# A two-block network on one core: activation chunks of the matmul operands laid out at 1072 and 1088 bytes instead of 1024

## What is computed

```python
h = h + hybrid_mixer(rms_norm(h, norm_mix_g), w_in, ..., w_out)
h = h + memory_cross_attention(rms_norm(h, norm_xa_g), rms_norm(mem, norm_mem_g), xa_wq, xa_wk, xa_wv, xa_wo)
h = h + squared_relu_mlp(rms_norm(h, norm_mlp_g), mlp_w1, mlp_w2)      # D_FF = 8192
...                                                                    # second block, other weights
x = x + gt1 * (concat([o_mla, o_na, o_fn]) @ w_out)
x = x + gt2 * conv_ffn(h2, w_up, conv_w, conv_b, w_down)               # D_FF_2 = 5632
```

## Time and profile before

| | |
|---|---|
| time, median of 3 runs | 3139.58 us (3137.08 to 3141.41) |
| the profiled execution | 3139.84 us, span 3138.0 us |
| TensorE busy, matmul and weight load | 2968.9 us (95%) and 2905.4 us (93%) |
| VectorE busy | 2101.9 us (67%) |
| ScalarE busy | 1331.6 us (42%) |
| mean granted TensorE clock | 0.971 |
| bytes moved, mean rate | 591.58 MB, 189 GB/s |

### The profile page before, as it was taken

The page is one execution under the profiler, slowest core; times in us unless marked ns, Lnnn a source line. Parts: engine busy times, 40 slices in busy tenths (PEclk is TensorE's granted clock), DMA queues, the critical chain, the costliest instruction groups (busy, mean ns, idle before and its releaser), DMA issues.

```text
span 3138.0 us, 55206 instructions
## 1 busy us (share of the span) xinstructions
PE 2968.9 (95%) x23858; PEld 2905.4 (93%) x23858; DVE 2101.9 (67%) x2934; ACT 1331.6 (42%) x1646; POOL 5.1 (0%) x13
## 2 busy tenths in 40 slices
PE   7999788999999899999999989979998999999998
PEld 7999788999998899999999979959498999999998
DVE  6988654688877777676776775445456665665565
ACT  3445323343433443444435444435344444444443
POOL 0000000000000000000000000000000000000000
PEclk9999898999999999999999989998899999999999
DMA  5555102577655677777777734514054555556553
GB/s 199 176 174 162 54 1 103 175 268 256 242 202 182 245 277 276 276 280 264 282 268 262 280 133 168 182 61 134 21 181 144 180 194 186 185 188 195 182 188 115
DMA packets 160451, 591.58 MB, mean 189 GB/s; under 512 B 17840, under 2 KB 17840, under 8 KB 159696
## 3 DMA queue, kind: packets, MB, share of 16 engines
q1 hardware_dynamic: 159264, 579.93, 53.2%
q0 software_dynamic: 944, 8.12, 0.7%
HBM read 585.88 MB, written 2.10 MB: 187 GB/s over the span
## 4 chain that ended last, share of the span: by engine, by line
PE 87%; DVE 9%; ACT 3%; issue 1%; DMA 0%; SPq 0%; DVEq 0%; ACTq 0%
PE bank L446 77%; DVE wlo L1216 2%; PE bank L710 1%; DVE ev L1235 1%; DVE modacc L1421 1%; PE bank L467 1%; PE bank L461 1%; PE bank L614 1%; DVE tmp L1371 1%; PE bank L471 1%; PE bank L612 1%; PE bank L606 1%; PE bank L685 1%; DVE ev L1338 1%; ACT whi L821 1%
## 5 line engine op out<-in xcount | busy, mean ns | idle before, releaser
L446 PE MATMUL bank<-act,whi 128*128 128x256 f32 x10144 | 1856.5, 286 | 54.3 <-DVE wlo L1216 15.3
L446 PEld LDWEIGHTS bank<-act,whi 128*128 128x128 f32 x10144 | 1603.9, 195 | 59.2 <-issue 33.7
L1216 DVE TENSOR_TENSOR wlo<-raw,whi 128x1024 fp32r<-128x1024 f32 x906 | 1102.2, 1223 | 572.0 <-ACT whi L821 565.6
L446 PE MATMUL bank<-act,wlo 128*128 128x256 f32 x5072 | 1446.9, 285 | 0.0
L821 ACT ACTIVATE whi<-raw 128x1024 fp32r<-128x1024 f32 x906 | 948.1, 1057 | 946.3 <-PE bank L446 944.1
L446 PEld LDWEIGHTS bank<-act,wlo 128*128 128x128 f32 x5072 | 986.3, 194 | 0.0
L446 PE MATMUL bank<-hid,whi 128*128 128x256 f32 x3456 | 597.1, 278 | 0.0
L446 PEld LDWEIGHTS bank<-hid,whi 128*128 128x128 f32 x3456 | 524.7, 188 | 0.0
L446 PE MATMUL bank<-hid,wlo 128*128 128x256 f32 x1728 | 480.0, 278 | 0.0
L1202 DVE SCALAR_TENSOR_TENSOR modacc<-modraw,small,modacc 128x512 f32<-128x512 f32 x480 | 348.2, 746 | 11.8 <-DMA modraw<-mods 6.6
L446 PEld LDWEIGHTS bank<-hid,wlo 128*128 128x128 f32 x1728 | 324.8, 188 | 0.0
(11 more groups left out here) (269 smaller groups left out, 1520.8 us busy)
## 6 DMA issues: line engine op xcount, KB each, us to landing
raw<-stream SPq DMA_DIRECT2D x906, 512.0 KB, 4.4
modraw<-mods SPq DMA_DIRECT2D x192, 512.0 KB, 4.2
h<-x_t SPq DMA_DIRECT2D x4, 512.0 KB, 6.8
memV<-mem_t POOLq DMA_DIRECT2D x1, 2048.0 KB, 9.3
tmp<-ctx_t POOLq DMA_DIRECT2D x1, 2048.0 KB, 12.2
out_t<-tmp SPq DMA_DIRECT2D x4, 512.0 KB, 2.6
cz<-catt POOLq DMA_DIRECT2D x1, 1216.0 KB, 12.9
bias<-na_bias POOLq DMA_DIRECT2D x1, 1024.0 KB, 5.5
```

The lines of the kernel that those rows point to most:

```text
L446: mm = pe.matmul(b[:, hf * T:(hf + 1) * T], lhs, rhs, start=(kc == 0 and hf == 0 and n == 0), stop=(kc == ph.chunks - 1 and n == 2), skip_ ...
L1216: ve.tensor_tensor(wlo[:, at % SPL_N, :], raw[:, at % RAW_N, :], whi[:, at % SPL_N, :].bitcast(F32), ALU.subtract).then_inc(split_done, 1)
```

## The change

Three tensors get another shape. `act` has 268 columns in place of 256 for each chunk, `hid` has 272, and both are then cut to the first 256, so that all code that uses them is as it was; a chunk now starts 1072 bytes after the one before it in `act`, and 1088 bytes in `hid`. `act` takes 1536 bytes more of each partition, `hid` 2048, and `small` takes 256 less, which its users don't reach. No instruction is added or removed; every tensor behind `act` moves by 1536 bytes, and every one behind `small` by 1280.

```diff
-        act = sb("act", [P, 2, DC, T], F32R)
+        act = sb("act", [P, 2, DC, T + 12], F32R)[:, :, :, 0:T]
...
-        small = sb("small", [P, 256])
+        small = sb("small", [P, 192])
...
-                hid = sb("hid", [P, 2, DC, T], F32R, stack=mlp)
+                hid = sb("hid", [P, 2, DC, T + 16], F32R, stack=mlp)[:, :, :, 0:T]
```

## The result

The changed kernel takes 3120.58 us (median of 5, 3120.2 to 3123.64), the kernel before beside it 3137.08 us. The ratio is 0.9947, with a 95% interval of 0.9933 to 0.9962: 0.5% faster, 17 us, where I had forecast 65. It lies inside the stated range of 3032 to 3152 and on the forecast side of no change, but the gain is a quarter of what was predicted.

The account below looks back on a forecast made before the run. TensorE's matmul pace, set by operand addresses, was taken to bound the kernel. Gains of 55.9, 7.2 and 1.6 us on `act`, 0 for `hid` and the rest, sum to 64.7: 3139.8 to 3075 us, range 3032 to 3152.

Parts of the forecast that it names:

- What bounds the kernel: Line 446 matmuls: TensorE, 95% busy, sets the time; 120 ns on `act`, 113.3 or 117.5 on `hid`, by operand addresses.
- The pace on `act`: Line 446 matmuls on `act`: 120 ns falls to 115 with the new stride, 55.9 us less over 466 slots.
- I take no change: `hid` slots in `w2` and `down`: new stride and start cost 0 us, between 15 us less and 19 more.
- VectorE as the next bound: 224 `act` slots: VectorE binds from 86 to a little over 90% busy, so only 7.2 and 1.6 us gained.
- Half are bad: Cost goes by distance modulo 128 or so; `act` 117.5, `hid` about 117: 3111 us; 0.15 together with VectorE's rival.
- VectorE takes it back: TensorE at 115 ns, but VectorE or ScalarE binds in more phases: half the gain, 3108 us; 0.15 shared.
- Nothing: Operand place doesn't make the 120 ns, or it goes by distance modulo 64: time stays 3140 us; chance 0.11.
- Slower: the changing distance breaks the step: Load and matmul streams never settle: 4.2 ns more a matmul, 70 us on `act`, 14 on `hid`: 3223 us; 0.14.
- All distances but 0 are good: Only 0 modulo 512 is bad; `act` and `hid` both run at 113.3 ns: 100 us less, 3040; chance 0.12.

Follow-up runs that it names:

- the scan: Kernel without the network, only line 446's weight loads and matmuls, 168 at each fixed operand distance: 113.3 to 120.0 ns a matmul over 16 places, mean 117.9.
- the kernel with distance 112: Against the kernel before: chunk strides of 1024 bytes kept, `act` starts 112 bytes later, `hid` 48, both at distance 112 modulo 256; 3039.22 us, ratio 0.9683.

## Why the prediction was right and wrong

**What bounds the kernel: right.** TensorE's pace by operand address carried 15.2 of the 17.2 us; both strides moved the pace, and no other engine's busy time changed by more than 1.2 us.

**The pace on `act`: mis-sized.** The step that failed is "I take 115. It is nearer to the `hid` rows since that is the one distance that isn't 0". It is 118.4, near the upper of the two values that I had from rows. The trace of before had two distances, 0 and 448, and these are one of the three worst and one of the two best of 16. I took the good one for the usual one. The pattern visits all 16 places equally often, so it gets their mean, 117.9 in the scan, and half a nanosecond for the short stay. At 118.4 the term of the sum is 466 x 24 x 1.6 ns = 17.9 us, and those phases measured 19.4. The step from slots to time was sound; the pace that went into it was not.

**`hid`: "I take no change" was wrong.** I had the bounds -15 and +19 and it was +10.8 (3.2 in `w2`, 7.6 in `down`). The row at hand said that `hid` stood well and that the change moves 12 of its 16 chunks off that place (modulo 256; by the modulo 512 of the prediction it is 14); the four places that it visits now have 113.3, 120.0, 117.8 and 118.7 in the scan, a mean of 117.4, and 117.0 was measured. Taking the middle of a range was no reading of the row. The bounds were off too: the 2.84 us of a slot in `w2` hold the line-461 matmuls, and I set them against slots without any. With 113.3 throughout, in the kernel with distance 112, `w2` is 8.0 us shorter and `down` the same, so the lower bound was -8; the upper one, with 120 ns throughout, is about +27 by the same paces, an estimate.

**VectorE as the next bound: wrong for most of the 224 slots.** I gave `glu`, `z`, `memk`, `memv` and `wq` less than half of the gain and `wo` nearly none, because VectorE was busy for 86 to 90% of a window. For `wo` I had misread the row. The window of the earlier trace rows runs to 1060, and `wo` ends at 1056:

```profile
1000.00:1056.00 56.00, 56.00 (x470) 55.95 (x468) 50.49 (x64) 21.09 (x22) 0.00 (x0) 1.00 0.74 253
1056.00:1060.00 4.00, 1.21 (x10) 0.97 (x8) 2.14 (x4) 0.90 (x2) 0.00 (x0) 1.00 0.96 387
```

All the 2.79 us in which TensorE stood still lie behind the phase, so that row shows no bound by VectorE. Whole phases say the same. `wo`, from its first to its last matmul, in the kernel before and in the one with distance 112:

```profile
958.70:1056.00 97.30, 97.26 (x800) 97.22 (x800) 85.96 (x108) 36.34 (x38) 0.00 (x0) 0.98 0.69 243
```

```profile
938.50:1029.30 90.80, 90.69 (x800) 90.50 (x799) 85.17 (x109) 36.16 (x38) 0.00 (x0) 1.00 0.73 261
```

The same 800 matmuls (32 of them are short ones of line 461), 6.5 us less or 0.20 us a slot, where the pace alone gives 0.16; the rest, 1.4 us, is a shorter wait in its first slot. VectorE goes from 88% to 94% of the phase. `glu` and `z` gave 0.10, `memk` and `wq` 0.16. Only `qkv` kept its time, 0.7 us less in 48 slots. From 60 to 280 us of the kernel before, ScalarE waited longest for this:

```profile
ACT qkvT L858 <- DVE ev L1235: 51.0, 11, 5.6
```

There ScalarE and VectorE hand a bank to each other, and ScalarE's next split stands behind that wait. So `qkv` was bound with VectorE at 86%; that this chain is the cause is my reading of the waits and the code, and no run takes it apart. So the share didn't tell the phases apart. At 118.4 ns this error was small (6.7 us gained in those 224 slots where my shares at that pace would give about 3), and it partly made up for the `hid` term.

**The rivals.** "Half are bad" came nearest, at 3111 with 117.5 for `act` and 117 for `hid` against the measured 118.4 and 117.0; I gave it 0.15 together with "VectorE takes it back". I had argued its mechanism by "modulo 128 or so", and the scan shows 256. "Nothing", which rested on the rule of the Trainium skill ("TensorE: Matmul & The Clock Gate", Part 2) that a weight load takes no read bandwidth from the running matmul, falls: with all other engines idle the pace goes from 113.3 to 120.0 by where the two operands stand, and it matters where the load's own operand starts. So the place has an effect. Whether it is read bandwidth that one takes from the other is not shown: that the two reads meet in the memory is a guess of mine, and no run here shows what happens inside. "Slower: the changing distance breaks the step" falls for `act`, whose patterns cost 0.4 ns by changing. The two paces of the earlier trace rows that it was built on are real: they are the two states of place 192. In the `w2` windows of the changed kernel there is no second pace, perhaps because no chunk stays at 192 for long; no run tests that. "All distances but 0 are good" falls by the scan, where 14 of 16 places are slower than 113.3. "VectorE takes it back" falls as well: it needed TensorE at 115, and in `up_1` TensorE never stood still and had 118.4.

**The sum.** Forecast were 55.9 us for the 466 slots, 8.8 for the other 224 on `act`, and 0 for `hid`. Measured are 19.4 (36 less, by the pace: 17.9 at 1.6 ns for 55.9 at 5), 6.7, and -10.8; with 2.0 between the phases that is 17.2, but for rounding. So the time landed in the range by a pace on `act` that gave a third of its term, less a loss on `hid` that I had put at nothing.

## What to carry to other kernels

When two operands of one matmul stream come from buffers at a fixed distance, measure the pace at several distances before laying anything out: here a scan of 16 places in one short run was worth more than the whole trace, which held two. A rotating stride buys the mean of all places (117.9 ns); a constant place that the scan shows as good and steady buys the best (113.3 ns), with 160 bytes and no instruction changed. And look at each place more than once with something different in front, since a place can have two steady paces.

## What the runs showed of the hardware that I had not expected

- With the load's operand on a multiple of 512 bytes, the pace of weight load and 256-column matmul in float32r depends on the byte distance of their operands modulo 256, from 113.3 to 120.0 ns on 16-byte steps and up to 123.4 ns on 4-byte steps, with no other engine busy.
- At distance 192 the same addresses run at 113.3 or 117.8 ns until something comes between; the four one-column matmuls of line 461 (two passes each) turned 113.3 into 117.8 in every round of `w2` before. What picks the state isn't known. At distance 112 only 113.3 was seen, in 8 groups, and it held through the long phases of the kernel, line-461 matmuls and all.
- The distance isn't the whole rule: with the load at 16 bytes and the matmul at 128 the pace is 120.0 ns, with 0 and 112 it is 113.3, at the same distance.
